# Latent attention with the keys on the partitions: a softmax down the partitions in place of one along the rows

## What is computed

```python
MLA_SCALE = (NOPE_B + ROPE_B) ** -0.5

def mla_attend(qn, qr, kn, kr, v):
    s = (jnp.einsum('bqhd,bkhd->bhqk', qn, kn, preferred_element_type=jnp.float32)
         + jnp.einsum('bqhr,bkr->bhqk', qr, kr, preferred_element_type=jnp.float32)) * MLA_SCALE
    p = jax.nn.softmax(s, axis=-1)
    o = jnp.einsum('bhqk,bkhd->bqhd', p.astype(v.dtype), v)
    return o.reshape(qn.shape[0], qn.shape[1], H_B * V_B)
```

## Time and profile before

| | us |
|---|---|
| span of the profiled execution | 3312.2 |
| median of the three timed executions | 3315.0 |
| PE busy | 3117.9 (94%) |
| DVE busy | 1331.6 (40%) |
| ACT busy | 780.3 (24%) |
| POOL busy | 621.2 (19%) |

### The profile page before, as it was taken

One profiled execution on the slowest core, in us unless ns is written; L12 is line 12 of the kernel. 1 busy time (PEld: TensorE's weight loads), 2 busy tenths in 40 slices (PEclk: granted clock), 3 DMA queues, 4 the chain that ended last, 5 costly groups with the idle time before them and its releaser, 6 DMA issues. The chain is left out here.

```text
span 3312.2 us, 35441 instructions
## 1 busy us (share of the span) xinstructions
PE 3117.9 (94%) x14154; PEld 1647.6 (50%) x14154; DVE 1331.6 (40%) x2223; ACT 780.3 (24%) x1548; POOL 621.2 (19%) x519
## 2 busy tenths in 40 slices
PE   7998989999949999599999988999999999999998
PEld 3457656665424444244456656444444444444443
DVE  2226437673351111524322465314525444544233
ACT  3126534442211111312212036111011211111001
POOL 0005400000000110023022125322203232321323
PEclk9999999999969999699999999999999999999999
DMA  7210000003267885501000130012101111113443
GB/s 287 76 51 29 1 26 1 1 1 155 115 249 295 331 332 174 202 32 38 29 24 27 52 134 2 32 51 95 70 38 51 51 39 39 50 38 141 137 132 130
DMA packets 65826, 311.38 MB, mean 94 GB/s; under 512 B 10240, under 2 KB 11776, under 8 KB 51840
## 3 DMA queue, kind: packets, MB, share of 16 engines
q1 hardware_dynamic: 61056, 292.35, 23.6%
q0 software_dynamic: 4608, 16.78, 2.0%
HBM read 272.39 MB, written 36.70 MB: 93 GB/s over the span
## 5 line engine op out<-in xcount | busy, mean ns | idle before, releaser
L2697 PE MATMUL banks<-hT,ffn_ring 128*128 128x512 f32 x528 | 235.7, 596 | 1.1 <-PEq L2393 1.1
L2857 PE MATMUL banks<-down_ring,down_sums 128*128 128x512 f32 x440 | 189.2, 592 | 0.0
L2697 PEld LDWEIGHTS banks<-hT,ffn_ring 128*128 128x128 f32 x528 | 101.0, 192 | 128.4 <-issue 128.3
L822 PE MATMUL banks<-kT_b,qT_b 96*128 96x512 f32 (+1 forms) x384 | 158.7, 523 | 3.5 <-ACT prob_b L884 2.4
L2697 PE MATMUL banks<-ffn_row_sums,ffn_w_sums 128*128 128x512 f32 x352 | 158.3, 592 | 1.2 <-DVE ffn_row_sums L2737 1.2
L330 PE MATMUL banks<-w_in,hT 128*128 128x512 f32 (+1 forms) x384 | 157.5, 567 | 1.2 <-PEq L157 1.2
L2747 DVE SCALAR_TENSOR_TENSOR ffn_acc<-ffn_u,s_ffn_taps,ffn_acc 128x1023 f32<-128x1023 f32 x88 | 125.0, 1421 | 68.0 <-ACT ffn_acc L2730 66.4
L2857 PEld LDWEIGHTS banks<-down_ring,down_sums 128*128 128x128 f32 x440 | 83.6, 190 | 105.2 <-issue 103.8
L728 POOL TENSOR_TENSOR prob<-prob,softmax_columns 128x640 f32<-128x640 f32 (+1 forms) x64 | 75.4, 1199 | 312.4 <-DVE softmax_columns L686 312.4
L1592 PE MATMUL banks<-hT,side_ring 128*128 128x512 f32 x256 | 127.5, 617 | 1.3 <-PEq L2208 1.3
L2666 POOL TENSOR_TENSOR ffn_w_sums<-ffn_ring 128x512 f32<-128x512 f32 x22 | 35.1, 1596 | 473.8 <-DMA ffn_ring<-in_w_ffn 344.2
(11 more groups left out here) (509 smaller groups left out, 5379.4 us busy)
## 6 DMA issues: line engine op xcount, KB each, us to landing
down_ring<-in_w_down SPq DMA_DIRECT2D x132, 256.0 KB, 2.9
expert_wg<-in_w_gate SPq DMA_DIRECT2D x16, 2048.0 KB, 15.4
expert_wu<-in_w_up SPq DMA_DIRECT2D x16, 2048.0 KB, 20.8
expert_wd<-in_w_down SPq DMA_DIRECT2D x16, 2048.0 KB, 8.5
ffn_ring<-in_w_ffn SPq DMA_DIRECT2D x22, 1024.0 KB, 4.8
wmod_slab<-in_w_mod SPq DMA_DIRECT2D x6, 2048.0 KB, 7.9
wmod_ring<-in_w_mod SPq DMA_DIRECT2D x4, 2048.0 KB, 10.9
w_out<-in_w_out SPq DMA_DIRECT2D x4, 2048.0 KB, 8.5
```

Source lines behind the costliest of these rows:

```text
L822: last = nc.tensor.matmul(scores(u)[:, a:b], heads[u // 2].q[u % 2], heads[u // 2].keys[u % 2][:, a:b], start=True, stop=True, skip_group_ ...
L2697: last = nc.tensor.matmul(product(f, m), wt[:, q, :], x[:, q, :], start=q == 0 and m != 2, stop=q == 3, skip_group_check=True)
L2857: last = nc.tensor.matmul(c.bank(4 - 4 * (p % 2) + t), stationary[:, P * t:P * t + P], w[s % RING][:, 0, :], start=j == 0, stop=j == N - 1)
```

## The change

`attend_by_keys` takes the place of `attend_latent`. A unit is now a pair of heads and 256 queries: 16 units, each worth four of the old ones. The scores are made turned, with 128 keys on the partitions and 2 x 256 queries along the row, one bank per key tile, ten key tiles (`score`). So the probabilities come out in the form in which the mix needs them, and are not transposed. What a softmax needs across the keys lies across partitions now:

- ACT copies each score tile into SBUF (`evict`, 128 x 512, ten per unit).
- DVE takes the maxima of tile against tile (`highest`: four instructions of 128 x 1024, one of 128 x 512), both operands in SBUF.
- PE transposes that tile of maxima (`turn`, 4 pieces), DVE reduces it to 4 columns (`highest_of`), PE spreads these over all partitions with 4 more transposes (`spread_max`, bank 5).
- DVE adds the negated maxima to all scores (`shift`: five instructions of 128 x 1024, one operand in SBUF, the other in bank 5), ACT makes the exponents in place (`exponents`, five of 128 x 1024).
- POOL adds up the exponents tile against tile (four of 128 x 1024, one of 128 x 512, all operands in SBUF), PE sums over the partitions by 4 matmuls with a column of ones (`total`), DVE inverts the 4 columns (`invert`), PE spreads them (`spread_inverse`), and DVE copies them out and multiplies the product by them (`take`). The probabilities themselves are not normalized.
- `mix` has two matmuls of 256 columns per key tile, one per head, each on its half of the array's columns.

The lists go in steps `g` of one key tile, ten per unit: PE has the scores of tile g and the mix of tile g - 14. The transposes of the maxima of a unit stand in step 0 of the next, behind its first score.

Besides, the first half of `w_out` goes to another place (on the keys of the first heads), and SP issues its load when half of the scores are made; and in `mix_and_route` DVE clears `aff` behind the first eight `mixed` steps, not ahead of them.

The core of the diff; the constructor of the new class `Query` and the body of the old function, which is printed above, are left out:

```diff
-def attend_latent(c, k, name, heads, bufs, before=None):
...
+def attend_by_keys(c, k, name, units, bufs, before=None):
...
+    prob, acc, top, col = bufs
+    n, QB, LAG = len(units), 2 * P, 14
+    END = NK * n + LAG + 5
+    half = lambda x: x.rearrange("p (e m) -> p e m", e=2)
...
+    def score_bank(g):
+        return c.bank(g % 4)
+    def tile(u, j):
+        return prob[:, u % 2, j, :]
+    def tiles(u, i):
+        return prob[:, u % 2, 2 * i:2 * i + 2, :]
+    def product(u):
+        return c.bank(6 + u % 2)
+    with nc.Block(no_gpsimd_drain=True) as block:
+        @block.sync
+        def _(sp):
+            before(sp, scored)
+        @block.tensor
+        def _(pe):
+            def score(u, j):
+                g = NK * u + j
+                if g >= 4:
+                    pe.wait_ge(evicted, g - 3)
+                for e in range(2):
+                    last = nc.tensor.matmul(score_bank(g)[:, QB * e:QB * e + QB], units[u].keys[e][:, P * j:P * j + P], units[u].q[e],
+                                            start=True, stop=True, skip_group_check=True)
+                last.then_inc(scored, 1)
+            def turn(u):
+                pe.wait_ge(maxed, 5 * u + 5)
+                if u:
+                    pe.wait_ge(negmax, u)
+                for i in range(4):
+                    last = nc.tensor.transpose(c.bank(4)[:, P * i:P * i + P], top[:, 0, P * i:P * i + P], k.ident[:, :])
+                last.then_inc(turned, 1)
+            def spread_max(u):
+                pe.wait_ge(negmax, u + 1)
+                if u:
+                    pe.wait_ge(shifted, 5 * u)
+                for i in range(4):
+                    last = nc.tensor.transpose(c.bank(5)[:, P * i:P * i + P], col[:, u % 2, 0, i:i + 1].to_broadcast([P, P]), k.ident[:, :])
+                last.then_inc(spread, 1)
+            def mix(u, j):
+                pe.wait_ge(exped, 5 * u + j // 2 + 1)
+                if j == 0 and u >= 2:
+                    pe.wait_ge(taken, u - 1)
+                for e in range(2):
+                    last = nc.tensor.matmul(product(u)[64 * e:64 * e + 64, 0:QB], units[u].values[e][j], tile(u, j)[:, QB * e:QB * e + QB],
+                                            start=j == 0, stop=j == NK - 1, skip_group_check=True)
+                last.then_inc(mixed, 1)
+            def total(u):
+                pe.wait_ge(summed, 5 * u + 5)
+                if u == 0:
+                    pe.wait_ge(ready, 1)
+                for i in range(4):
+                    last = nc.tensor.matmul(product(u)[:, QB + i:QB + i + 1], acc[:, u % 2, 0, P * i:P * i + P], k.one[:, :],
+                                            start=True, stop=True, skip_group_check=True)
+                last.then_inc(totalled, 1)
+            def spread_inverse(u):
+                pe.wait_ge(inverted, u + 1)
+                for j in range(2):
+                    for e in range(2):
+                        last = nc.tensor.matmul(product(u)[64 * e:64 * e + 64, QB + P * j:QB + P * j + P],
+                                                col[:, u % 2, 1, 2 * e + j:2 * e + j + 1].to_broadcast([P, 64]), k.ident[:, :],
+                                                start=True, stop=True, skip_group_check=True)
+                last.then_inc(spread_back, 1)
+            for g in range(END):
+                u, j = divmod(g, NK)
+                if u < n:
+                    score(u, j)
+                if j == 0 and 1 <= u <= n:
+                    turn(u - 1)
+                if j == 1 and 1 <= u <= n:
+                    spread_max(u - 1)
+                if 0 <= g - LAG < NK * n:
+                    mix(*divmod(g - LAG, NK))
+                v, i = divmod(g - LAG - NK, NK)
+                if i == 1 and 0 <= v < n:
+                    total(v)
+                if i == 3 and 0 <= v < n:
+                    spread_inverse(v)
+        @block.vector
+        def _(dve):
+            nc.vector.memset(k.one[:, :], 1.0).then_inc(ready, 1)
+            def highest(u, i):
+                dve.wait_ge(evicted, NK * u + 2 * i + 2)
+                if i == 1:
+                    if u:
+                        dve.wait_ge(turned, u)
+                    nc.vector.tensor_tensor(top[:, :, :], tiles(u, 0), tiles(u, 1), ALU.max).then_inc(maxed, 1)
+                else:
+                    dve.wait_ge(maxed, 5 * u + i - 1)
+                    nc.vector.tensor_tensor(top[:, :, :], top[:, :, :], tiles(u, i), ALU.max).then_inc(maxed, 1)
+                if i == 4:
+                    dve.wait_ge(maxed, 5 * u + 4)
+                    nc.vector.tensor_tensor(top[:, 0, :], top[:, 0, :], top[:, 1, :], ALU.max).then_inc(maxed, 1)
+            def highest_of(u):
+                dve.wait_ge(turned, u + 1)
+                if u >= 2:
+                    dve.wait_ge(spread, u - 1)
+                nc.vector.reduce_max(col[:, u % 2, 0, :], c.bank(4).rearrange("p (i m) -> p i m", i=4), AX.X, negate=True).then_inc(negmax, 1)
+            def shift(u, i):
+                if i == 0:
+                    dve.wait_ge(spread, u + 1)
+                if i < 2:
+                    dve.wait_ge(maxed, 5 * u + 1)
+                nc.vector.tensor_tensor(tiles(u, i), tiles(u, i), c.bank(5).unsqueeze(1).to_broadcast([P, 2, 2 * QB]), ALU.add).then_inc(shifted, 1)
+            def invert(u):
+                dve.wait_ge(totalled, u + 1)
+                if u >= 2:
+                    dve.wait_ge(spread_back, u - 1)
+                nc.vector.reciprocal(col[:, u % 2, 1, :], product(u)[:, QB:QB + 4]).then_inc(inverted, 1)
+            def take(u):
+                dve.wait_ge(spread_back, u + 1)
+                dve.wait_ge(mixed, NK * u + NK)
+                nc.vector.tensor_copy(k.inverse[:, :], product(u)[:, QB:2 * QB]).then_inc(taken_one, 1)
+                dve.wait_ge(taken_one, u + 1)
+                nc.vector.tensor_tensor(units[u].out, product(u)[:, 0:QB], k.inverse[:, :], ALU.mult).then_inc(taken, 1)
+            for g in range(END):
+                u, j = divmod(g, NK)
+                if j == 0 and 1 <= u <= n:
+                    highest_of(u - 1)
+                if 1 <= u <= n and j % 2:
+                    shift(u - 1, j // 2)
+                if u < n and j % 2 and j > 1:
+                    highest(u, j // 2)
+                v, i = divmod(g - LAG - NK, NK)
+                if i == 2 and 0 <= v < n:
+                    invert(v)
+                if i == 4 and 0 <= v < n:
+                    take(v)
+        @block.gpsimd
+        def _(pool):
+            for u in range(n):
+                for i in range(1, 5):
+                    pool.wait_ge(exped, 5 * u + i + 1)
+                    if i == 1:
+                        if u >= 2:
+                            pool.wait_ge(totalled, u - 1)
+                        nc.gpsimd.tensor_tensor(acc[:, u % 2], tiles(u, 0), tiles(u, 1), ALU.add).then_inc(summed, 1)
+                    else:
+                        pool.wait_ge(summed, 5 * u + i - 1)
+                        nc.gpsimd.tensor_tensor(acc[:, u % 2], acc[:, u % 2], tiles(u, i), ALU.add).then_inc(summed, 1)
+                pool.wait_ge(summed, 5 * u + 4)
+                nc.gpsimd.tensor_tensor(acc[:, u % 2, 0, :], acc[:, u % 2, 0, :], acc[:, u % 2, 1, :], ALU.add).then_inc(summed, 1)
+        @block.scalar
+        def _(act):
+            def evict(u, j):
+                g = NK * u + j
+                act.wait_ge(scored, g + 1)
+                if u >= 2:
+                    act.wait_ge(mixed, NK * (u - 2) + j + 1)
+                    act.wait_ge(summed, 5 * (u - 2) + max(j // 2, 1))
+                nc.scalar.activation(tile(u, j), score_bank(g), ACT.Identity).then_inc(evicted, 1)
+            def exponents(u, i):
+                act.wait_ge(shifted, 5 * u + i + 1)
+                nc.scalar.activation(tiles(u, i), tiles(u, i), ACT.Exp).then_inc(exped, 1)
+            for g in range(END):
+                u, j = divmod(g, NK)
+                if u < n:
+                    evict(u, j)
+                if j % 2 == 0:
+                    v, i = (u - 1, j // 2 - 1) if j else (u - 2, 4)
+                    if 0 <= v < n:
+                        exponents(v, i)
...
@@ -983,16 +1045,19 @@
     groups = [([k.b_tok[:, t, h, :] for t in ts], k.kT_b[:, h, P * ts[0]:P * ts[0] + P * len(ts)], None, None)
               for ts in ([0, 1, 2, 3], [4, 5, 6, 7], [8, 9]) for h in range(HB)]
     transpose_groups(c, "turn_kb", groups, k.ident)
-    bufs = (c.area("prob_b", F + 5440, 3, NK * P), c.area("probT_b", F + 9280, 2, 2, NK * P), c.area("softmax_columns_b", F, 4, 3, 2))
-    heads = [Pair([k.qT_b[:, 2 * i + e, P * qt:P * qt + P] for e in range(2)], [k.kT_b[:, 2 * i + e, :] for e in range(2)],
-                  [[k.v_b[:, t, 64 * (2 * i + e):64 * (2 * i + e) + 64] for t in range(NK)] for e in range(2)],
-                  k.OT[:, 4 + i, P * qt:P * qt + P]) for i in range(HB // 2) for qt in range(NT)]
```

(21 more changed lines are left out.)

114 lines of the change are left out of this document (4 added, 110 removed).

## The result

The changed kernel takes 3434.57 us (median of four runs, 3427.95 to 3451.13) against 3315.5 for the kernel before in the same comparison (3314.1 to 3316.87). The ratio is 1.0365, with a 95% interval from 1.0338 to 1.0393: slower, by 119 us. The four runs come in the order of their mean granted clocks of PE: 3427.95 us at 0.961, 3428.17 at 0.960, 3440.97 at 0.955, 3451.13 at 0.951. The profiled execution is the one of 3428.17 us, with a span of 3426.4; what the two longer ones did is in no trace. Ratios further down are to the kernel before, too.

What follows compares the result with a forecast made beforehand. PE was taken to bound the old stretch (303.6 us). The new one, 11.4 + 15 x 25.2 + 19.2 = 408.6 us, adds 105, plus 1 behind it: 3420 us, slower; range 3330 to 3450, main case 3395 to 3450.

Steps and rivals of the forecast that it cites:

- PE sets the pace before, with 18.56 us per four units: Old latent attention: PE busy all the time, 4.64 us per old unit, 4 x 4.64 = 18.56 us per new unit.
- PE's work 18.15 us: PE's own work per new unit: ten steps of 1.59 us plus transposes, totals and spreading, 18.15 us against 18.56.
- the round trip: PE going to half-array work and back, once per step: 0.30 us each, ten per unit where four stood.
- Prices of POOL and DVE: Per operation of 1024 elements: POOL's sum 2.35 us (ends 1.97 and 2.5), DVE's maximum or shift 1.22 us.
- The exclusion, and who goes first: DVE's maxima and POOL's sums block each other; POOL's fourth sum precedes the short maximum, so PE idles 5.3 us per unit.
- the case that the short maximum goes first: Rival: DVE's short maximum precedes POOL's fourth sum; maxima end at 21.2, period 22.4 us, time 3378 us; chance 0.20.
- The clock, 1.7 us, with 0 and 2.7 as ends: Loss per unit from PE working at half clock behind its idle gap: 1.7 us, with 0 and 2.7 as ends.
- Period 25.2: Time per new unit: 23.5 us until the short maximum is done plus 1.7 us of clock loss, 25.2 us.
- Ends: Stretch outside the 15 periods: 11.4 us at the start, 19.2 us from the last maxima on.
- the second: Rival: POOL and DVE do not exclude each other; PE idles 1.3 us per unit, no clock lost, 3335 us; chance 0.12.
- The third: Rival: no price for array-mode changes and no exclusion; 16.5 us per unit, faster, 3289 us; chance 0.06.
- The fourth: Rival: longer half-clock stretches or a second wait of PE per unit; above 3450 us; chance 0.08.

Runs made afterwards that it cites:

- `turn_later`: Changed kernel with the transposes of the maxima, and all that follows them, two steps later, the mix 16 tiles behind instead of 14: 3324.87 us, ratio 1.0031.
- `pool_waits`: Changed kernel, but POOL's fourth sum of a unit waits until the short maximum of the next unit is done: 3411.04 us, ratio 1.0289.
- `filled_gap2`: Changed kernel plus ten matmuls of 256 columns, results never read, ahead of PE's wait for the maxima, in 14 of 16 units: 3399.77 us, ratio 1.0256.
- `quiet_pool`: Changed kernel with POOL's additions replaced by one-column fills, so the sums are constants and the output is not normalized: 3335.06 us, ratio 1.0063.
- `half_and_bank`: `turn_later` with each score matmul split over the array's halves, and DVE's maxima taken from the score banks with one SBUF operand: 3284.69 us, ratio 0.9905.
- `short_end`: `half_and_bank`, but for the last unit POOL adds only six tiles and PE takes the other four in its one-column matmuls: 3284.99 us, ratio 0.9906.
- `half_scores`: `turn_later` with each score matmul split into two of 64 keys, one on each half of the array's columns: 3338.74 us, ratio 1.0066.

## Why the prediction was right, and where its terms were off

The forecast was 3420 us and slower, against 3434.6, inside its range. By its own steps:

- **PE sets the pace before, with 18.56 us per four units.** The runs fit it: where PE does not wait in the new kernel (`turn_later`), its work of 18.64 sets the period, and the time is that of the kernel before plus 0.3%.
- **PE's work 18.15 us.** Too low by 0.5: it is 18.64. The term mis-sized is the round trip. The step was forecast at 1.59 us, with 0.30 for the trip; it takes 1.64, and 1.30 without the trip, so 0.34. Ten steps of 0.05 make the 0.5. The forecast that PE's work falls slightly was therefore of the wrong sign: it rises by 0.1 us. So even a kernel without any wait would not have gained by this order.
- **Prices of POOL and DVE.** POOL's sum of 1024 was taken as 2.35, between ends of 1.97 and 2.5: 2351 to 2368 ns. DVE's shift as 1.22: 1.21, and so for the maximum when nothing is beside it (1225 ns). ACT 0.60 and 1.06: 0.60 and 1.05.
- **The exclusion, and who goes first.** The walk put POOL's fourth sum ahead of the short maximum by 0.3 us; it was 0.2 in the unit shown, and the order was so in all units but the first (sixteen short maxima, only one of them at 0.69). The gap of PE was forecast at 5.3 and is 4.61, or 4.83 with the pipeline's end. As the margin was seen as thin, the case that the short maximum goes first was given 0.20; `pool_waits` is that case, made on purpose. Its gap was 2.59, or 2.8 with the pipeline's end, where the walk gives 21.2 - 18.2 = 3.0; its time was 3411 and not 3378, by the two long stretches at half clock and by more work.
- **The clock, 1.7 us, with 0 and 2.7 as ends.** 2.25, by `filled_gap2`. The reading of the earlier trace rows was right, that a gap of several us is followed by a stretch at 0.50; the size taken was that of the shorter one, and in turn the longer one came.
- **Period 25.2.** 25.73. More work (0.4 above the 18.2 of the walk) and more clock loss (0.55) stand against a shorter wait (0.5). That the period came out so near is in part luck: one error took back half of the two others.
- **Ends.** Start 11.4: 11.5 (483.37 to the first transposes at 494.92). Between, 15 x 25.2 = 378: 381.0. Here, too, errors cancel: fourteen periods were 0.5 us longer each, 7 in all, and the first one, whose missing mixes the forecast left out of account, was 4.4 shorter. End 19.2: 22.2. It was added up at full clock, and the window from 875.93 has a clock of 0.73: the transposes, reduction and spreading took 3.2 and not 2.1, the totals, inverse and taking 4.2 and not 2.9. POOL's five sums took 11.2 and not 10.7. For the start of `mix_and_route` 1 us was taken: PE is at 0.50 there up to about 905.6, 5.7 us of its work, where it was 3.4 in the earlier trace rows; by that 1.2 us are lost more than before (an estimate), and 1.5 is what the part behind the stretch grew by.
- **Span and median.** 3312.2 + 106 = 3418.2 was worked out for the span, and it is 3426.4. The rest is not in the trace: the median lies 8.2 us above the span, where 2.8 were carried over, since two of the four runs had a lower clock than the profiled one.

Of the rivals, the second (no exclusion, 3335 us) is refuted by L869's 2483 ns against L885's 1208; DVE and POOL do exclude each other here. That `quiet_pool`, in which POOL reads nothing, took 3335.06 is a coincidence: its period was 19.89 and not 19.45, and its end, without POOL's sums, 15.1 us (788.66 to 803.79) and not 19.2. The third (no price for round trips either, 3289 us) is refuted by the step of 1.64; `half_and_bank`, in which both prices are taken away by hand, gives 3284.69. The fourth did not come.

So the added 119 us are, per unit and in the order in which the runs took them away: 3.59 us by the exclusion (23.48 - 19.89, 54 us over 15 units), 2.25 by the clock (34 us), 1.25 by the place of the transposes (19.89 - 18.64, 19 us). The other 13 are 1 of PE's work (18.64 against 18.56), 4 at the ends of the stretch, 3 outside it, and 5 by which the median lies further above the span than before. The division is by these runs, and another order of taking away could give other shares: the terms act on each other, as `turn_later` shows, which takes away all three by one move.

## What to carry to other kernels

When work is given to an idle GpSimd, look at the operands, not only at busy shares: with both inputs of DVE's operation in SBUF the two engines take turns, and a chain of dependent DVE operations can lose its place between two links; one operand from a bank avoids it. Before fewer matmul passes are counted as a gain, count the changes between whole and half array (0.34 us per round trip here), and see whether the rest can be split into halves as well. And put an instruction that waits behind enough other work on its engine: a gap costs by its length, and can cost again by the clock (2.25 us per gap of 4.61 here, nothing at 1.03).

## What the runs showed of the hardware that was not expected

- In `pool_waits` PE stayed at 0.50 for two stretches of 37.5 us in which it was busy all the time, while the same gap of 2.59 us was followed in other units by a much shorter stretch at 0.50, and in three of them by none (the units from 562.25, 606.77 and 732.96 took 21.4 us at a clock of 1.00). So one gap's length alone does not tell what the clock does behind it. The Trainium skill's page "TensorE: Matmul & The Clock Gate", section What's actually happening, says that activity releases the throttle; these two stretches do not agree with it. With a gap of 1.03 us per unit (`quiet_pool`) or none, the clock stayed full.
- Matmuls of one column without a pause did not keep the clock up: in `short_end` it went from full to 0.50 at 747.6 us, 2.8 us after they began. Ahead of them were gaps of 1.1 us between mixes, so whether these gaps or the matmuls brought it down stays open.
- Making PE faster made the kernel slower (`half_scores` against `turn_later`, 3338.74 against 3324.87), since which of DVE and POOL is first hangs on a few tenths of a microsecond.
